# Issuing each modulation piece two weight transfers later on SyncE in a two-layer transformer trunk

## The reference

```python
for i in range(DEPTH):                              # DEPTH = 2
    mod = (silu(c) @ w_ada[i] + b_ada[i])           # w_ada[i]: 2048 x 12288
    sh_a, sc_a, g_a, sh_m, sc_m, g_m = split(mod, 6)
    h = x * (1 + sc_a) + sh_a
    y = diff_attention(h, ...) if i == 0 else sliding_window_attention(h, ...)
    x = layer_norm(ALPHA * x + (1 + g_a) * y, ...)
    h = x * (1 + sc_m) + sh_m
    y = square(relu(h @ w_up[i])) @ w_down[i]       # 2048 -> 8192 -> 2048
    x = layer_norm(ALPHA * x + (1 + g_m) * y, ...)
```

## Time and profile before

| | before |
|---|---|
| median of 3 runs (lowest to highest) | 2228.6 us (2226.92 to 2228.74) |
| the profiled execution, its own time | 2228.67 us |
| its span | 2226.9 us |
| TensorE busy | 2168.5 us, 97% |
| VectorE busy | 1790.6 us, 80% |
| ScalarE busy | 981.3 us, 44% |
| DMA, mean over the span | 268 GB/s |
| 0.5 MiB pieces into `ada_w`, issue to landing | 6.1 us (median of 320) |

### The profile page before, as it was taken

How to read it: one execution, slowest core, us unless ns; L and a number is a source line. 1 busy time by engine, 2 the same in 40 slices (tenths; PEclk the granted TensorE clock), 3 DMA queues, 4 the chain that set the end, 5 groups by cost and what they waited for, 6 DMA issues and landing times.

```text
span 2226.9 us, 26022 instructions
## 1 busy us (share of the span) xinstructions
PE 2168.5 (97%) x9952; PEld 1791.8 (80%) x9952; DVE 1790.6 (80%) x2057; ACT 981.3 (44%) x1330; POOL 33.4 (2%) x53
## 2 busy tenths in 40 slices
PE   6999999999999999999999999999999999999997
PEld 6887888877888888888888788777888888888886
DVE  6899998887997897888786888777966865874877
ACT  1135444546433443443353655536534443443441
POOL 0001000000000000000000000000000000000000
PEclk9899999999999999999999999999999999999999
DMA  9999888877999999999985643365766676666663
GB/s 360 384 331 347 322 320 300 306 245 256 361 364 325 354 366 335 325 380 350 323 311 190 198 152 119 122 207 190 236 221 223 213 241 206 219 217 219 228 234 113
DMA packets 262592, 596.41 MB, mean 268 GB/s; under 512 B 13426, under 2 KB 14788, under 8 KB 262468
## 3 DMA queue, kind: packets, MB, share of 16 engines
q1 hardware_dynamic: 254800, 579.45, 74.2%
q10 hardware_dynamic: 7668, 15.30, 2.2%
HBM read 592.60 MB, written 2.10 MB: 267 GB/s over the span
## 4 chain that ended last, share of the span: by engine, by line
PE 88%; DVE 7%; DMA 1%; issue 1%; ACT 1%; SPq 0%; DVEq 0%; POOL 0%; ACTq 0%; POOLq 0%
PE pair L1709 25%; PE pair L1711 25%; PE pair L1710 25%; DVE acc L916 2%; DVE w_lo L901 1%; PE pair L1967 1%; PE pair L1969 1%; PE pair L1968 1%; PE pair L1729 1%; PE pair L1731 1%; PE pair L1730 1%; PE turn L2041 1%; DMA y<-in_w_ada_dram 1%; PE turn L2022 1%; PE turn L1603 1%
## 5 line engine op out<-in xcount | busy, mean ns | idle before, releaser
L528 ACT ACTIVATE w_hi<-raw 128x1024 fp32r<-128x1024 f32 x712 | 726.8, 1056 | 620.2 <-PE pair L1711 297.4
L901 DVE TENSOR_TENSOR w_lo<-raw,w_hi 128x1024 fp32r<-128x1024 f32 x712 | 852.5, 1220 | 117.0 <-ACT w_hi L528 110.8
L1709 PE MATMUL pair<-w_hi,h_hi 128*128 128x512 f32 x1456 | 581.3, 399 | 1.5 <-DVE w_lo L901 0.8
L1711 PE MATMUL pair<-w_hi,h_lo 128*128 128x512 f32 x1456 | 567.8, 390 | 0.0
L1710 PE MATMUL pair<-w_lo,h_hi 128*128 128x512 f32 x1456 | 567.3, 390 | 0.0
L1709 PE MATMUL pair<-w_hi,f_hi 128*128 128x512 f32 x1056 | 414.0, 392 | 0.1
L1711 PE MATMUL pair<-w_hi,f_lo 128*128 128x512 f32 x1056 | 411.1, 389 | 0.0
L1710 PE MATMUL pair<-w_lo,f_hi 128*128 128x512 f32 x1056 | 410.9, 389 | 0.0
L929 DVE SCALAR_TENSOR_TENSOR acc<-ada_w,cvec,acc 128x1024 f32<-128x1024 f32 x300 | 383.6, 1279 | 1.8 <-DVE x L1312 0.9
L1709 PEld LDWEIGHTS pair<-w_hi,h_hi 128*128 128x128 f32 x1456 | 273.5, 188 | 62.9 <-DVE w_lo L901 6.3
L1711 PEld LDWEIGHTS pair<-w_hi,h_lo 128*128 128x128 f32 x1456 | 273.2, 188 | 58.4
(11 more groups left out here) (190 smaller groups left out, 1669.5 us busy)
## 6 DMA issues: line engine op xcount, KB each, us to landing
ada_w<-in_w_ada_dram SPq DMA_DIRECT2D x320, 512.0 KB, 6.1
raw<-in_w_up_dram SPq DMA_DIRECT2D x128, 1024.0 KB, 6.1
raw<-in_w_down_dram SPq DMA_DIRECT2D x128, 1024.0 KB, 5.2
raw<-in_a_w_qkv_dram SPq DMA_DIRECT2D x48, 1024.0 KB, 7.6
ada_f<-in_w_ada_dram SPq DMA_DIRECT2D x44, 512.0 KB, 11.5
raw<-in_b_w_qkv_dram SPq DMA_DIRECT2D x20, 1024.0 KB, 5.2
raw<-in_a_w_o_dram SPq DMA_DIRECT2D x16, 1024.0 KB, 6.5
raw<-in_b_w_o_dram SPq DMA_DIRECT2D x16, 1024.0 KB, 5.1
```

The lines of the kernel that those rows point to most:

```text
L528: act.activation(w_hi[:, (b.n * SUB + n) % SPLITS], raw[:, slot, k:k + 2], ACT.Copy).then_inc(hi_ready, 1)
L901: dve.tensor_tensor(w_lo[:, slot, k:k + 2], raw[:, slot, k:k + 2], w_hi[:, (b.n * SUB + n) % SPLITS].bitcast(F32), ALU.subtract).then_inc( ...
L1709: pe.matmul(o, hi[:, kt, at], w[:, k], start=kt == 0, stop=False)
L1711: mm = pe.matmul(o, lo[:, kt, at], w[:, k], start=False, stop=kt == KT - 1)
```

## The change

SyncE keeps a short list of counts. After each quarter it appends how many pieces belong to that quarter, and fetches as many as the quarter two before it called for. The pieces keep their order, and so do the quarters; what VectorE adds, and when in its own order, is the same. All pieces behind the first two go through `load_block`, so the shift holds for 318 of the 320. The order of instructions on the other four engines is the same, row for row.

```diff
+ADA_LAG = 2
...
-            def load_block(src, ada=(), ada_of=None):
+            due = deque([0] * ADA_LAG)
+
+            def load_block(src, ada=()):
 
                 b = st.block
                 for q in range(Q):
                     load_raw(Q * b.n + q, src(q))
-                    for n in ada:
-                        if n // 2 == q:
-                            load_ada(ada_of())
+                    due.append(sum(n // 2 == q for n in ada))
+                    for _ in range(due.popleft()):
+                        load_ada(ada_src(*next(pieces)))
                 b.n += 1
...
-            tiles_a = iter([ada_src(0, part, half, kt) for part in (2, 3, 4) for half in range(2) for kt in range(KT)])
...
+            parts = [(0, 2), (0, 3), (0, 4), (1, 0), (1, 1), (1, 3), (1, 4), (0, 5), (1, 2), (1, 5)]
+            pieces = ((layer, part, half, kt) for layer, part in parts for half in range(2) for kt in range(KT))
...
-                load_block(qkv_a(i % 3 * D + i // 3 * NC), ADA_A[PIECES_A[i]], of_a)
+                load_block(qkv_a(i % 3 * D + i // 3 * NC), ADA_A[PIECES_A[i]])
```

More of the change, by code:

```diff
@@ L1 @@
 import math
+from collections import deque
 from contextlib import ExitStack
@@ L407, in load_block @@
                     load_raw(Q * b.n + q, src(q))
-                    for n in ada:
-                        if n // 2 == q:
-                            load_ada(ada_of())
+                    due.append(sum(n // 2 == q for n in ada))
+                    for _ in range(due.popleft()):
+                        load_ada(ada_src(*next(pieces)))
                 b.n += 1
-            def half_stream(layer, part, half):
-                k = iter(range(KT))
-                return lambda: ada_src(layer, part, half, next(k))
-            tiles_a = iter([ada_src(0, part, half, kt) for part in (2, 3, 4) for half in range(2) for kt in range(KT)])
-            def of_a():
-                return next(tiles_a)
+            parts = [(0, 2), (0, 3), (0, 4), (1, 0), (1, 1), (1, 3), (1, 4), (0, 5), (1, 2), (1, 5)]
+            pieces = ((layer, part, half, kt) for layer, part in parts for half in range(2) for kt in range(KT))
             def load_x(j):
@@ L460, in _ @@
             for _ in FIRST_ADA:
-                load_ada(of_a())
+                load_ada(ada_src(*next(pieces)))
             st.block.n += 2
@@ L476, in _ @@
             for i in range(2):
-                load_block(paired(a_w_o[0], i), ADA_A[PIECES_A[12 + i]], of_a)
+                load_block(paired(a_w_o[0], i), ADA_A[PIECES_A[12 + i]])
             for j in range(2, NCH):
-                load_block(lambda q: w_rows(a_w_o[0], q * 4 * P, j * NC), ADA_A[PIECES_A[12 + j]], of_a)
+                load_block(lambda q: w_rows(a_w_o[0], q * 4 * P, j * NC), ADA_A[PIECES_A[12 + j]])
             def mlp(layer):
@@ L489, in mlp @@
                 load_block(up(0, 0))
[L490 to L494, removed]
                 for b in range(8 * QUARTERS - 1):
@@ L498, in mlp @@
                     src = up(it, i + 1) if i < 3 else down(it, i - 3) if i < 7 else up(it + 1, 0)
-                    load_block(src, mlp_pieces(b, 2 * len(parts)), of)
+                    load_block(src, mlp_pieces(b, MLP_HALVES[layer]))
             mlp(0)
```

## The result

| | before | after |
|---|---|---|
| median (lowest to highest, runs) | 2228.67 us (2226.92 to 2229.05, 4) | 2244.35 us (2241.04 to 2247.23, 4) |
| the profiled execution, its own time; span | 2228.67; 2226.9 us | 2243.2; 2241.4 us |

The ratio is 1.0071, with an interval of 1.0054 to 1.0089. The change made the kernel 15.7 us slower by the medians and 14.5 us by the spans. I had forecast 2230.0, within 2226.5 to 2236.5: the result lies outside.

The account below looks back on a forecast made before the run. The prediction took TensorE, busy 97% of the span, to bound the kernel. Terms of +1.1 us at block 4 and +0.3 at block 13 added +1.4 to 2228.67, giving 2230.0 us, range 2226.5 to 2236.5.

Parts of the forecast that it names:

- What bounds the kernel, and the queue: Whole kernel: TensorE bounds it; the queue's 685.9 us wait for VectorE falls under 350, its wait for TensorE rises about equally.
- Faster and starved TensorE: Faster: 1.6 us gain at most, 0.03 past the edge; TensorE starved in the first MLP: 2280 us and up, 0.02.
- Step 1: Start of the attention, pieces 4 to 17: estimated in time or at most 0.8 us late.
- Step 2: Block 4, subtile 2: piece 18 lands 1.1 us late and delays TensorE's turn behind the gate addition, +1.1 us.
- Step 3: Rest of the attention: single pieces slip 0 to 3.6 us, within the combinations' slack of 2.6 to 4.7; no cost.
- Step 4: Block 13, end of the attention: piece 87 lands 4.9 us late, idle time takes up most, +0.3 us.
- Step 5: Block 15: piece 95, the last of a sum TensorE takes up right behind it, at most 0.5 us late; nothing counted.
- Step 6: First MLP, 192 pieces: the latest slips 3.4 us, a typical late one leaves 5.2 us before TensorE needs `w_lo`; no cost.
- a rival for the MLP: Limited stream rate in the MLP: backlog grows 0.4 us a quarter to 1.6, sum some +2.2 us; no chance given.
- Step 7: Second MLP, 32 pieces: late by up to 3.7 us, only where VectorE has little else to do; no cost.
- The rival of late landings: Attention: landings 1.5 us longer than estimated give +4.4 us, 2.5 us longer +8.4; chance 0.12 past the edge.
- The signs of being wrong: VectorE's waits passed to TensorE in first MLP; attention pieces landing over 9 us after their quarter's issue; TensorE's norm waits going.

## Why the prediction was wrong

*What bounds the kernel, and the queue*: right. The wait of 685.9 us went to 28.9 and the wait for TensorE rose by 636 us, with no gain. Faster and starved TensorE were rightly given little.

*Step 1, start of the attention*: right, nothing was lost before piece 18.

*Step 2, piece 18, +1.1*: the right piece and the right place, and the wrong size, 7.2 us. This term missed by more than any other. Two things were missing from it. Its landing was 9.2 us from its own issue (9.6 by the median of its bundle), by ScalarE's 512 KB load; I had looked at SyncE's queue alone for what else moves bytes, and with the load out of the way the term measured 1.4. And the price of a wait was taken as its length, where the clock added 2.7 us to 4.5. The slack of 1.1 us at the turn was read rightly, and did not help: the gate addition behind it has none, so all of the lateness reached TensorE there.

*Step 3, the rest of the attention, "Nothing"*: this is the step whose mechanism failed. I held late pieces against the combinations alone. VectorE also hands back the place of the modulation vector in block 11, 0.25 us before TensorE wants it, and a place of the same kind, the gate's, was the critical one in my own step 2. It cost 4.8 us, of which 1.6 are clock, and block 8 another 0.5. Making TensorE ask three subtiles later took the loss at block 11 to nothing.

*Step 4, block 13, +0.3*: nothing was lost.

*Step 5, block 15, at most 0.5 late*: 0.7 us, and 1.9 to 2.4 in the four kernels of the study whose clock fell there, behind a wait of 0.23 to 0.28 us.

*Step 6, first MLP, "Nothing"*: almost. 192 pieces cost 2.7 us in the profiled execution, 2.2 of them at block 19, mostly by two loads on ScalarE's queue; I had named blocks 17 to 22 as those where pieces land in time. Bundle by bundle the median landing grew there from 6.6 us (issued at 547 to 549) to 11.6 (563 to 566) and was 7.8 again from 575 to 600, which is a backlog of the kind that I had set out as a rival for the MLP, though it did not last. Whether the rate of the stream makes it was not tried. The limit of 358 GB/s on a core's HBM, which the Trainium skill gives (DMA: Bandwidth & Descriptors, specifications), is not what bounds it: the row at block 11 shows 388 GB/s over 5 us, and the stretch from 575 to 580 us, behind the slowest bundles, 407.

*Step 7*: right, nothing is lost behind block 41.

*The rival of late landings* had the right kind and sign, at 0.12. With landings 2.5 us longer throughout it gave +8.4. In the attention they were 0.3 to 0.4 us over my estimate by the median and some 3.5 over it at piece 18. In the first MLP they were 1.5 us over as a rule (from 600 to 1230 us the medians are 7.7 and 9.0 us from the quarter's issue, the longest 12.7), and that cost TensorE only 0.5 us behind block 20: the cover that step 6 counted was there. The rival's price lacked block 11 and the clock.

*The signs of being wrong*: two of the three showed. Pieces 18 and 19 landed 9.7 and 11.0 us after their quarter's issue, and VectorE's waits were passed on in the first MLP, at block 19. TensorE's waits at norms did not go.

## What to carry to other kernels

Before an engine's transfers are ordered later, list every place where the bound engine takes something back from the engine that will be late, freed places included, with the slack at each: a place with 0.25 us of slack appears in no wait list. Look for bytes on every engine's queues around each late transfer. And allow for a price above a wait's length, without counting on it: here waits of 3.2 and 4.5 us brought 1.6 and 2.7 us of slower matmuls behind them, one of 3.06 us brought none, and one of 0.25 us brought 1.4.

## What the runs showed of the hardware

- The granted clock fell to its lower level behind two waits in a row, of 3.42 and 1.82 us, and behind 2.04 and 1.82. It did not behind 0.25 and 1.82. With the gap filled by small matmuls it did not fall either.
- The length of the wait does not decide it alone. At block 11 it fell behind 2.99 us and not, in the kernel with the gate bias early, behind 3.06. At block 19 it fell behind 1.97 us in the kernel with the sum later and not behind 1.98 in the changed one. Before block 15's sum it fell behind 0.23 to 0.28 us in four kernels and not behind 0.27 in the changed one. What else decides was not tried.
- A load of 512 KB on ScalarE's queue, issued 4.0 us ahead of the pieces of a bundle of 2 MiB on SyncE's, made them land 3 us later (9.6 for 6.4 us), and 1.8 to 3.1 us later in four other kernels. Two of 256 KB issued right behind a bundle added 2.1 us (11.9 for 9.8).
- Alone on the queue a quarter of 1 MiB lands in 5.1 us (4.9 to 5.5), where my rate gave 4.7; by the fit of the Trainium skill's page on DMA (DMA: Bandwidth & Descriptors, section on the anatomy of one DMA) the estimate would be 4.4.
